# Projections of the second (HGRN2) layer: from float32 matmuls to three float32r products per weight tile

## The chip, the cores and the metric

One NeuronCore of a Trainium2 chip runs the whole program in one launch. The metric is the device time of one execution in microseconds. Five engines work in parallel, each on its own list of instructions, and meet at semaphores: PE (matrix multiply), DVE (VectorE), ACT (ScalarE), POOL (GpSimd) and SP, which here only issues transfers.

## The reference, cut to what matters

The reference chains four layers: an attention/convolution layer, an HGRN2 layer (below called layer 2), and a second block of two layers with feed-forward parts. The change touches the input projections of layer 2: 512 latent tokens and 256 context tokens of width 1024.

```python
def c_layer(x, xc, mod, mod_c, w_in, w_out, lb_f, lb_b, g_norm, ln_g, ln_b, ctx_out):
    widths = (C_F_WIDTH, C_F_WIDTH, C_F_WIDTH, C_I_WIDTH, C_I_WIDTH)      # five times 1024
    q, zf, zb, i, g = split_cols(modulate(x, shift, scale) @ w_in, widths)
    zfc, zbc, ic = split_cols(hc @ w_in[:, C_F_WIDTH:3 * C_F_WIDTH + C_I_WIDTH], ...)
    q = jax.nn.silu(to_heads(q, C_KEY_DIM)) * (C_KEY_DIM ** -0.5)
    o_f, oc_f = hgrn2_direction(q, i, zf, lb_f, qc, ic, zfc, ctx_out, reverse=False)
    o_b, oc_b = hgrn2_direction(q, i, zb, lb_b, qc, ic, zbc, ctx_out, reverse=True)
    y = hgrn2_readout(o_f + o_b, g, g_norm, w_out)
    x_new = layer_norm(DEEPNORM_ALPHA * x + gate * y, ln_g, ln_b)
```

`hgrn2_direction` takes log f = log sigmoid(z), its running sums along the tokens, and from their exponentials the keys, decays and scores of a linear recurrence, for 8 heads in both directions.

## The kernel before, in words

Tokens lie in tiles of 128; `HT` ("acts" in the profile) holds the modulated input transposed, 8 slices of 128 features by 768 tokens, and `X` ("resid") the residual rows. Weights come in chunks of 1024 x 256 float32 (1 MB) into `WR` ("weights_raw"), a ring of three slots; SP fills a slot when the chunk three places earlier is released.

Where this kernel already splits a product (the first layer, the second block), ACT or DVE rounds a chunk to float32r ("weights_hi"), POOL subtracts it from the raw chunk in place ("weights_lo"), and PE sums three products: hi by hi, hi by lo, lo by hi. The projections of layer 2 are not split before the change: one float32 matmul for each slice of 128 features. The trace records such a matmul as two.

Layer 2 has one step for each of the 8 heads (`STEPS`; two heads share a chunk of q or i). The projections are cut in units: `z` of a head has three (forward gate, backward gate, both for the context tokens), `q` two, `i` three, `g` two. In step `st` PE computes the three `z` units of the next head and two or three units of q, i or g, laid by halves between the recurrence's own work by `c_slots`: `between(0)` to `between(7)`. That work on PE is, in this order: transposes of the keys (L1084, "kt"), level 0 (L1013), `between(0)`, the outputs of the head before (L1020, L1033), states (L1099), the diagonal (L1107), level 1, `between(1)`, level 2, `between(2)`, then levels 3 to 6 with `between(3)` to `between(6)` behind them.

A level is a chain over four engines: POOL makes its arguments (`level_args`, three instructions, L2998 to L3000), ACT their exponential (L1673), DVE multiplies by keys and queries (L2304, L2305), PE multiplies (L1013) and DVE merges the result under a mask. The arguments have two buffers, so `level_args` of a level waits until PE has read the level two before.

The next head's gates form a second chain through the same engines, which starts when the last `z` unit is complete: ACT copies it out of PSUM (L1624) and takes a sigmoid (`keys`), DVE takes |z| (L2260), ACT an exponential and a logarithm (L1641, L1647), DVE forms log f (L2267) and four running sums (scans, L2273 to L2276) and signals `hg_sums` (L2280), ACT takes exponentials of them (`state_factors`, L1660 to L1669), DVE multiplies them by the keys (L2286, "h_z") and signals `hg_ks`, on which PE's kt of the next step waits. Every engine runs its list in the written order.

Of the kernel before, what the change touches and what calls it, by code (L numbers as in the profile page):

```python
# [48 lines left out]
def table_layout():  # L49

    sizes = [("ident", P), ("ones", P), ("pick", 2), ("win_lo", P), ("win_hi", P), ("dil", 1280),
             ("lv", P * len(LEVELS)), ("rot_ax", P), ("rot_pt", P),
             ("cos_ax", L), ("sin_ax", L), ("chunk", L), ("cols", 6)]
    at, out = 0, {}
    for name, n in sizes:
        out[name] = (at, at + n)
        at += n
    return out, at


def make_tables():
# [9 lines left out]
    put("pick", i[:, None] % 32 == np.arange(2)[None, :])  # L71
# [53 lines left out]
def program(nc, a, out, stop=99):  # L125
    lay, tw = table_layout()
    ctx = ExitStack()
    with ctx:
# [55 lines left out]
        chunks = []  # L184
# [18 lines left out]
        TAB_FIRST = lay["pick"][1]  # L203
# [5 lines left out]
        PICK = tab("pick")  # L209
# [14 lines left out]
        HKS = view(w + 19456, L, name="h_keys")  # L224
# [3 lines left out]
        HO = view(hi_at, TL, D, name="h_out")  # L228
# [9 lines left out]
        def c_slots(st):  # L238
# [8 lines left out]
            if st == LAST:  # L247
                share = (2, 2, 2, 2, 2, 0, 0, 0)
            else:
                share = (2, 2, 2, 1, 0, 2, 1, 0) if len(units) == 5 else (2, 2, 2, 1, 1, 2, 2, 0)  # L250
# [61 lines left out]
        Y_HI, Y_LO = parts("ab_out_hi", ht_at, KD, LT), parts("ab_out_lo", w + 4608, KD, LT)  # L312
        C_HI = parts("c_out_hi", w + 4096, KD, L)
# [224 lines left out]
        def _(pe):  # L538
# [10 lines left out]

            def chunk(pieces, kt=KD):  # L550

                n = len(chunks)
                s = n % WSLOTS
                chunks.append((pieces, kt))
                wcount[s] += 16 * len(pieces)
                pe.wait_ge(wload[s], wcount[s])
                return WR[:, s]
# [31 lines left out]
            def split_chunk(name, pieces, kt=KD, by="a"):  # L589
# [5 lines left out]
                w_hi, w_lo = OWN_HI[name] if name in OWN_HI else W_HI[:, len(splits) % 2], W_LO[n % WSLOTS]  # L595
# [4 lines left out]
                splits.append((n % WSLOTS, kt, w_hi, wload[n % WSLOTS], wcount[n % WSLOTS], by, hi_done, len(hi_list)))  # L600
# [365 lines left out]
            c_weights, c_release = {}, {}  # L966
# [6 lines left out]
            def product_half(unit, half):  # L973

                kind, key, part = unit
                if half == 0:
                    if part == 0:
                        c_weights[kind, key] = chunk(c_pieces(kind, key))
                        c_release[kind, key] = len(released)
                        released.append((None, 0))  # L980
# [4 lines left out]
                wv = c_weights[kind, key]  # L985
                ps = obank[n % 2]
                if kind in "zq" and part < 2:
# [3 lines left out]
                elif kind == "z":  # L991
                    for k in range(KD):
                        last = pe.matmul(ps[:, half * LC:(half + 1) * LC], wv[:, k, half * P:(half + 1) * P], HT[:, k, L:LT],
                                         start=k == 0, stop=k == KD - 1)
                else:
                    t = 2 * part + half
                    for k in range(KD):
                        last = pe.matmul(ps[:, half * WC:(half + 1) * WC], HT[:, k, t * P:(t + 1) * P], wv[:, k, :],  # L998
# [4 lines left out]
                if part == C_PARTS[kind] - 1:  # L1003
                    released[c_release[kind, key]] = (sem("products_filled"), n + 1)

# [37 lines left out]
            def turn_heads(hb, ps):  # L1043

                pe.wait_ge(sem("c_y"), hb + 1)
                for j in range(HH):
                    for t in range(TL):
                        h = HH * hb + j
                        last = pe.transpose(ps[:, j * L + t * P:j * L + (t + 1) * P], HO[:, t, h * P:(h + 1) * P], IDENT)
# [7 lines left out]
            product(("q", 0, 0))  # L1057
            pe.wait_ge(*read_of("h1.4"))
# [3 lines left out]
            mod_next(14)  # L1062
            product(("i", 0, 0))
            mod_next(15)
            product(("i", 0, 1))
            product(("i", 0, 2))
            mod_turn(1, 11)
            for st, (hb, hj) in enumerate(STEPS):
# [23 lines left out]
                pe.wait_ge(*product_emptied(("i", hb, 2)))  # L1092
# [292 lines left out]
        def _(sp):  # L1385
# [6 lines left out]
            for n, (pieces, kt) in enumerate(chunks):  # L1392
                if n == 10:
                    sp.dma_start(TAB[:, TAB_FIRST:tw], a["tables"][:, TAB_FIRST:tw]).then_inc(sem("tables_in"), 16)
                if n >= WSLOTS:
# [1765 lines left out]
```

## Time and profile before

| | us |
|---|---|
| median of 3 runs (2344.57 to 2349.4) | 2348.21 |
| the profiled execution, its own time | 2346.51 |
| its span in the trace | 2344.5 |
| PE busy in the span | 2151.1 (92%) |
| DVE, POOL, ACT busy | 1063.8, 810.5, 668.5 |
| mean granted TensorE clock | 0.97 |

Layer 2 begins with the product at 505.6 us of the span, its first step at 567.1, and its output product at 1055.2. A row of the timeline has the start and the duration of one instruction or of a run of like ones, the engine, the line of the program, what it writes and reads, and in brackets how long the engine stood idle before it and whom it waited for. Ends of matmuls are modelled and overlap the next start, so the pace of a run of matmuls is read from starts.

### The profile page before, as it was taken

To read this page: it belongs to the slowest core of one execution; us is meant where nothing else is said; L and a number is where in the kernel's file an instruction comes from. 1 tells how busy PE (TensorE), PEld (TensorE's weight loads), DVE (VectorE), ACT (ScalarE), POOL (GpSimd) and SP (SyncE) were. 2 spreads that over 40 slices of the span, in tenths; PEclk is the share of its full clock that TensorE was granted. 3 is DMA by queue.
4 is the path that set the end of the run, shared out by engine and by line. 5 is a ranking of instruction groups with operands and counts; after the bars stand their busy time and mean duration, and the time that the engine had idled before them with its cause. 6 is when DMAs were issued, how large, how long until landed. Compare 5 with 4: busy or idle time off the path is not lost. (4 is left out here: it accounts for less than half of the span.)

```text
span 2344.5 us, 27285 instructions
## 1 busy us (share of the span) xinstructions
PE 2151.1 (92%) x11287; PEld 1717.0 (73%) x11287; DVE 1063.8 (45%) x1685; ACT 668.5 (29%) x1043; POOL 810.5 (35%) x429
## 2 busy tenths in 40 slices
PE   4999888989898989987898899999998999999998
PEld 3887777866575757776855678888887688888886
DVE  2113664663555555557995543111126684111114
ACT  3223223334545454642112432100113353000111
POOL 1421113311333333325500015553544234554453
PEclk7999999999999999999899999999999999999999
DMA  9242113433111111113111112322322222232332
GB/s 300 72 116 74 55 55 91 126 109 90 36 36 36 36 36 37 36 55 99 41 36 54 55 54 72 105 93 91 107 90 90 83 97 72 90 108 90 93 96 81
DMA packets 183114, 187.41 MB, mean 80 GB/s; under 512 B 25728, under 2 KB 162256, under 8 KB 182864
## 3 DMA queue, kind: packets, MB, share of 16 engines
q1 hardware_dynamic: 173040, 175.42, 24.4%
q10 hardware_dynamic: 9376, 8.16, 1.3%
q8 instruction: 90, 1.47, 0.3%
q0 software_dynamic: 576, 2.10, 0.2%
q14 instruction: 32, 0.26, 0.0%
HBM read 183.56 MB, written 2.10 MB: 79 GB/s over the span
## 5 line engine op out<-in xcount | busy, mean ns | idle before, releaser
L3011 POOL TENSOR_TENSOR weights_lo<-weights_raw,weights_hi 128x2048 fp32r<-128x2048 f32 (+1 forms) x101 | 457.6, 4531 | 865.5 <-ACT weights_hi L1429 669.4
L698 PE MATMUL ring<-input_hi,weights_hi 128*128 128x512 f32 x784 | 305.4, 390 | 4.1 <-POOL weights_lo L3011 4.1
L700 PE MATMUL ring<-input_hi,weights_lo 128*128 128x512 f32 x784 | 305.0, 389 | 0.0
L699 PE MATMUL ring<-input_lo,weights_hi 128*128 128x512 f32 x784 | 305.0, 389 | 0.0
L2837 DVE CAST weights_hi<-weights_raw 128x2048 fp32r<-128x2048 f32 (+1 forms) x72 | 87.7, 1218 | 366.2 <-PE ring L700 173.9
L2998 POOL TENSOR_TENSOR h_w<-h_p 128x512 f32<-128x512 f32 x56 | 73.6, 1314 | 381.9 <-PE ring L1013 265.1
L989 PE MATMUL obank<-acts,weights_raw 128*128 128x512 f32 x384 | 179.6, 622 | 0.0
L698 PEld LDWEIGHTS ring<-input_hi,weights_hi 128*128 128x128 f32 x784 | 147.2, 188 | 36.4 <-issue 5.9
L700 PEld LDWEIGHTS ring<-input_hi,weights_lo 128*128 128x128 f32 x784 | 147.2, 188 | 30.5
L699 PEld LDWEIGHTS ring<-input_lo,weights_hi 128*128 128x128 f32 x784 | 147.2, 188 | 30.4
L998 PE MATMUL obank<-weights_raw,acts 128*128 128x256 f32 x640 | 142.7, 380 | 0.0
L989 PEld LDWEIGHTS obank<-acts,weights_raw 128*128 128x128 f32 x384 | 75.6, 203 | 87.2 <-issue 87.1
L1346 PE MATMUL ring<-weights_hi,hidden_hi 128*128 128x512 f32 x352 | 136.9, 389 | 0.0
L1347 PE MATMUL ring<-weights_lo,hidden_hi 128*128 128x512 f32 x352 | 136.9, 389 | 0.0
L1348 PE MATMUL ring<-weights_hi,hidden_lo 128*128 128x512 f32 x352 | 136.9, 389 | 0.0
L998 PEld LDWEIGHTS obank<-weights_raw,acts 128*128 128x128 f32 x640 | 120.3, 191 | 16.3 <-issue 0.8
L2858 DVE TENSOR_TENSOR f_gate<-f_gate,ring 128x1024 f32<-128x1024 f32 x22 | 26.9, 1221 | 212.4 <-PE ring L700 212.4
L3114 POOL TENSOR_TENSOR hidden_lo<-f_gate,hidden_hi 128x1024 fp32r<-128x1024 f32 x22 | 52.6, 2391 | 162.3 <-ACT hidden_hi L1925 162.3
L1013 PE MATMUL ring<-h_w 128*128 128x128 f32 x448 | 65.9, 293 | 46.0 <-DVE h_w L2305 25.0
L1013 PEld LDWEIGHTS ring<-h_w 128*128 128x128 f32 x448 | 59.2, 201 | 60.8 <-DVE h_w L2305 34.0
L1673 ACT ACTIVATE h_w<-h_w 128x1024 f32<-128x1024 f32 x56 | 58.5, 1053 | 131.2 <-POOL h_w L3000 131.0
L1925 ACT ACTIVATE hidden_hi<-f_gate 128x1024 fp32r<-128x1024 f32 x22 | 23.4, 1063 | 246.8 <-DVE f_gate L2858 246.8
(465 smaller groups left out, 4429.2 us busy)
## 6 DMA issues: line engine op xcount, KB each, us to landing
weights_raw<-in_w_ada SPq DMA_DIRECT2D x24, 1024.0 KB, 5.4
weights_raw<-in_ffn_w_gate SPq DMA_DIRECT2D x22, 1024.0 KB, 5.4
weights_raw<-in_ffn_w_up SPq DMA_DIRECT2D x22, 1024.0 KB, 5.4
weights_raw<-in_ffn_w_down SPq DMA_DIRECT2D x16, 1024.0 KB, 5.0
weights_raw<-in_w_in_c SPq DMA_DIRECT2D x12, 1024.0 KB, 5.2
weights_raw<-in_w_in_ab SPq DMA_DIRECT2D x9, 1024.0 KB, 7.2
weights_raw<-in_w_in_c SPq DMA_DIRECT2D x16, 512.0 KB, 5.3
weights_raw<-in_ev_w_in SPq DMA_DIRECT2D x8, 1024.0 KB, 5.5
```

Source lines behind the costliest of these rows:

```text
L698: pe.matmul(o, hi[:, k, ms], xh[:, k, t0:t0 + n], start=k == 0, stop=False)
L699: pe.matmul(o, hi[:, k, ms], xl[:, k, t0:t0 + n], start=False, stop=False)
L700: last = pe.matmul(o, lo[:, k, ms], xh[:, k, t0:t0 + n], start=False, stop=k == KD - 1)
L989: last = pe.matmul(ps[:, 0:L], wv[:, k, part * P:(part + 1) * P], HT[:, k, 0:L], start=k == 0, stop=k == KD - 1)
L998: last = pe.matmul(ps[:, half * WC:(half + 1) * WC], HT[:, k, t * P:(t + 1) * P], wv[:, k, :], start=k == 0, stop=k == KD - 1)
L1013: last = pe.matmul(ps[:, cs], W[:, 0, cs], W[:, 1, cs], start=True, stop=True)
L1346: pe.matmul(o, F_HI[f // 2][:, f % 2, ts], hi[:, k, :], start=f == 0, stop=False, skip_group_check=True)
L1347: pe.matmul(o, F_HI[f // 2][:, f % 2, ts], lo[:, k, :], start=False, stop=False, skip_group_check=True)
L1348: last = pe.matmul(o, F_LO[f // 2][:, f % 2, ts], hi[:, k, :], start=False, stop=end, skip_group_check=True)
L2837: dve.tensor_copy(w_hi[:, 0:kt, :], WR[:, slot, 0:kt, :]).then_inc(done, 1)
L2998: pool.tensor_tensor(w4[:, :, :, 0, :], refs.to_broadcast([P, 2, n, h2]), p4[:, :, :, 0, :], ALU.subtract)
L3011: pool.tensor_tensor(W_LO[slot][:, 0:kt, :], WR[:, slot, 0:kt, :], w_hi[:, 0:kt, :], ALU.subtract).then_inc(sem("w_lo"), 1)
```

## The change

The projections of layer 2 become sums of three float32r products, except those of `z` of head 0 and of `q` of heads 0 and 1.

- Weights: 18 chunks (`C_SPLIT`). `c_weights_hi(i)` on ACT rounds chunk i. Chunks of even number (i, q, g) are always loaded into the slot of the first of them, those of odd number (z, later g) into a second slot; the third slot holds the high parts of the odd ones. The high parts of the even ones lie in the part of the output `HO` that is not yet filled, and from number 12 on in two other places. `c_weights_lo(i)` on POOL subtracts in place. `chunk` is cut into `reserve` and the wait, and each chunk records its slot, its arrival count and who held the slot.
- Inputs: DVE casts the six tiles of `HT` to float32r (`C_XH` over the latent rows of `X`, `C_XH2` over tables); low parts go into `HT` itself, tiles 0 and 1 by DVE, tiles 2, 3 and the context by POOL, once the unsplit products have read it.
- `X` is therefore written to DRAM (`x_kept`, POOL's queue, 2 MB) and read back (SP's queue) behind the second chunk of the output weights.
- The mask table of a later attention ("dil") is loaded in the second block, not at the start.
- The first three units of i change order (the context's first), and in the last step the units of g are spread as 1, 1, 2, 2, 2, 2 halves over `between(0)` to `between(5)`, before as 2, 2, 2, 2, 2.

```diff
+            def c_weights_hi(i):
+                n = c_chunk[C_SPLIT[i]]
+                for before in (c_before[:2], c_before[2:])[i] if i < 2 else (c_chunk[C_SPLIT[i - 2]],):
+                    act.wait_ge(*released[before])
+                act.wait_ge(wload[slot_of[n]], arrival[n])
+                for k0, k1, home in c_hi_homes(i):
+                    act.activation(home[:, :, :], WR[:, slot_of[n], k0:k1, :], ACT.Copy).then_inc(sem("c_w_hi"), 1)
...
+            def c_weights_lo(i):
+                s = slot_of[c_chunk[C_SPLIT[i]]]
+                pool.wait_ge(sem("c_w_hi"), c_parts_made(i))
+                for k0, k1, home in c_hi_homes(i):
+                    pool.tensor_tensor(W_LO[s][:, k0:k1, :], WR[:, s, k0:k1, :], home[:, :, :], ALU.subtract).then_inc(sem("c_w_lo"), 1)
...
                 for st in range(len(STEPS)):
                     more = st + 1 < len(STEPS)
                     for i in range(2, 7):
                         level_args(7 * st + i)
+                        if i == (3 if more else 2):
+                            c_weights_lo(2 * st + 2)
+                        if i == (6 if more else 5):
+                            c_weights_lo(2 * st + 3)
...
+            def split_half(unit, half, ps):
...
+                if kind in "zq" and part < 2:
+                    for k in range(KD // 2 * half, KD // 2 * (half + 1)):
+                        ms = slice(part * P, (part + 1) * P)
+                        pe.matmul(ps[:, 0:L], c_hi(i, k)[:, ms], C_XH[:, :, k, :], start=k == 0, stop=False)
+                        pe.matmul(ps[:, 0:L], c_hi(i, k)[:, ms], C_XL[:, k, 0:L], start=False, stop=False)
+                        last = pe.matmul(ps[:, 0:L], lo[:, k, ms], C_XH[:, :, k, :], start=False, stop=k == KD - 1)
...
             product(("z", 0, 2))
             product(("q", 0, 1))
             mod_next(14)
+            pe.wait_ge(sem("c_in_lo"), 1)
+            product(("i", 0, 2))
+            mod_next(15)
+            pe.wait_ge(sem("c_in_lo_v"), 2)
             product(("i", 0, 0))
-            mod_next(15)
+            pe.wait_ge(sem("c_in_lo"), 3)
             product(("i", 0, 1))
-            product(("i", 0, 2))
...
+                if n == x_back_after[0]:
+                    for t in range(TL):
+                        sp.wait_ge(sem(f"x_kept{t}"), 16)
+                        sp.dma_start(X[:, t, :], X_KEPT[t]).then_inc(sem(f"x_back{t}"), 16)
```

POOL's list at the end of a step (h_p holds the running sums, h_w the levels' arguments; the last three h_w rows are level 6, the ones behind them level 0 of the next head). Before:

```order
L2998 TENSOR_TENSOR h_w33_81<-h_p31_79 128x512 [waits psum_filled]
L2999 TENSOR_TENSOR h_w33_81<-h_p31_79 128x256
L3000 TENSOR_TENSOR h_w33_81<-h_p31_79 128x256
L2998 TENSOR_TENSOR h_w32_80<-h_p30_78 128x8x64 [waits psum_filled,hg_sums]
L2999 TENSOR_TENSOR h_w32_80<-h_p30_78 128x4x64
```

After:

```order
L3136 TENSOR_TENSOR h_w33_81<-h_p31_79 128x512 [waits psum_filled]
L3137 TENSOR_TENSOR h_w33_81<-h_p31_79 128x256
L3138 TENSOR_TENSOR h_w33_81<-h_p31_79 128x256
L3172 TENSOR_TENSOR weights_lo1_145<-weights_raw9_57,c_w_hi2_156 128x2048 [waits c_w_hi]
L3136 TENSOR_TENSOR h_w32_80<-h_p30_78 128x8x64 [waits psum_filled,hg_sums]
L3137 TENSOR_TENSOR h_w32_80<-h_p30_78 128x4x64
```

One subtraction of 128 x 2048 stands between level 6 and the next head's level 0.

ACT's list over the same stretch, from the exponential of |z| to the exponentials of the sums. Before:

```order
L1641 ACTIVATE h_t26_74<-h_t26_74 128x1536 [waits hg_abs]
L1673 ACTIVATE h_w32_80<-h_w32_80 128x1024 [waits hg_warg]
L1647 ACT_TABLE_LOAD
L1647 ACTIVATE h_t26_74<-h_t26_74,tables1_49 128x1536 [waits hg_small]
L1673 ACT_TABLE_LOAD
L1673 ACTIVATE h_w33_81<-h_w33_81 128x1024 [waits hg_warg]
L1628 ACTIVATE h_i37_85<-obank0 128x512 [waits products_filled]
```

After:

```order
L1751 ACTIVATE h_t26_74<-h_t26_74 128x1536 [waits hg_abs]
L1783 ACTIVATE h_w32_80<-h_w32_80 128x1024 [waits hg_warg]
L1757 ACT_TABLE_LOAD
L1757 ACTIVATE h_t26_74<-h_t26_74,tables1_49 128x1536 [waits hg_small]
L1783 ACT_TABLE_LOAD
L1783 ACTIVATE h_w33_81<-h_w33_81 128x1024 [waits hg_warg]
L1745 ACTIVATE c_w_hi2_156<-weights_raw9_57 128x2048 [waits weights1,products_filled]
L1729 ACTIVATE h_i37_85<-obank0 128x512 [waits products_filled]
```

The rounding of the odd chunk stands behind level 6's exponential.

DVE's list ahead of the first step, behind the first head's logarithm. Before:

```order
L2276 SCALAR_TENSOR_TENSOR h_p30_78<-h_t26_74,tables1_49 128x255
L2278 COPY small4_52<-h_p30_78 128x6 [waits dve_chain]
L2279 TENSOR_TENSOR small4_52<-h_p30_78,h_t26_74 128x6
L2280 COPY small4_52<-small4_52 128x12 [waits dve_chain]
L2286 TENSOR_TENSOR h_z24_72<-h_z24_72,h_k28_76 128x1536 [waits hg_exps,hg_k]
```

After:

```order
L2409 SCALAR_TENSOR_TENSOR h_p30_78<-h_t26_74,tables1_49 128x255
L2411 COPY small4_52<-h_p30_78 128x6 [waits dve_chain]
L2412 TENSOR_TENSOR small4_52<-h_p30_78,h_t26_74 128x6
L2413 COPY small4_52<-small4_52 128x12 [waits dve_chain]
L2385 TENSOR_TENSOR c_in_lo_153<-acts8_56,c_in_hi_151 128x8x128 [waits products_filled] x2
L2419 TENSOR_TENSOR h_z24_72<-h_z24_72,h_k28_76 128x1536 [waits hg_exps,hg_k]
```

The two input subtractions, for which PE's product of i (tiles 0 and 1) waits, stand behind the scans.

## Rows read from the trace of the kernel before

**Rows 1.** Windows: window, its us, each engine's busy us; steps 4 and 5

```profile
807.34:865.79 58.45, 51.65 (x215) 33.18 (x214) 31.32 (x42) 25.90 (x34) 20.85 (x21) 0.94 0.12 36
865.79:927.53 61.74, 55.68 (x279) 43.36 (x278) 37.95 (x52) 30.55 (x40) 22.68 (x22) 1.00 0.12 35
```

**Rows 2.** Waits of PE, 480 to 1060 us: total, times, longest

```profile
PE ring L1013 <- DVE h_w L2305: 25.0, 18, 3.3
PE ring L1013 <- DVE h_states L2342: 20.9, 8, 3.0
```

**Rows 3.** Timeline of PE: one float32 unit each, 512 and 256 columns

```profile
809.32 7.03 PE L989 MATMUL obank<-acts,weights_raw 128*128 128x512 f32 x16
835.35 7.07 PE L993 MATMUL obank<-acts,weights_raw 128*128 128x256 f32 x32
```

**Rows 4.** Timeline of PE: float32r matmuls elsewhere, 512 columns, then 256

```profile
1399.67 0.40 PE L638 MATMUL ring<-weights_hi,e_out_hi 128*128 128x512 f32 x1
...
1402.87 0.39 PE L640 MATMUL ring<-weights_hi,e_out_lo 128*128 128x512 f32 x1
...
419.95 0.28 PE L884 MATMUL ring<-weights_hi,ab_out_hi 128*128 128x256 f32 x1
...
422.35 0.28 PE L886 MATMUL ring<-weights_hi,ab_out_lo 128*128 128x256 f32 x1
```

**Rows 5.** Timeline of ACT in step 4

```profile
838.03 1.06 ACT L1673 ACTIVATE h_w<-h_w 128x1024 f32<-128x1024 f32 x1 [2.78 <-POOL h_w L3000]
842.45 0.60 ACT L1624 ACTIVATE h_z<-obank 128x512 f32<-128x512 f32 x1 [3.37 <-PE obank L993]
850.96 1.57 ACT L1647 ACTIVATE h_t<-h_t,tables 128x1536 f32<-128x1536 f32 x1
853.85 1.06 ACT L1673 ACTIVATE h_w<-h_w 128x1024 f32<-128x1024 f32 x1
858.38 0.21 ACT L1660 ACTIVATE small<-small 128x12 f32<-128x12 f32 x1 [3.48 <-DVE small L2280]
```

**Rows 6.** Timeline of DVE in step 4

```profile
852.57 1.76 DVE L2267 SCALAR_TENSOR_TENSOR h_t<-h_z,h_t 128x1536 f32<-128x1536 f32 x1 [0.71 <-ACT h_t L1647]
856.08 1.20 DVE L2275 TENSOR_TENSOR_SCAN h_p<-h_t,tables 128x511 f32<-128x511 f32 x1
857.20 0.66 DVE L2276 TENSOR_TENSOR_SCAN h_p<-h_t,tables 128x255 f32<-128x255 f32 x1
859.94 1.10 DVE L2305 TENSOR_TENSOR h_w<-h_w,h_q 128x512 f32<-128x512 f32 x1
862.90 2.38 DVE L2286 TENSOR_TENSOR h_z<-h_z,h_k 128x1536 f32<-128x1536 f32 x1 [1.21 <-ACT h_t L1669]
```

**Rows 7.** Timeline of PE in steps 4 and 5: levels 1 and 6, kt, level 4

```profile
824.95 1.69 PE L1013 MATMUL ring<-h_w 128*128 128x128 f32 x8 [2.79 <-DVE h_states L2342]
861.47 1.05 PE L1013 MATMUL ring<-h_w 128*128 128x128 f32 x8
865.79 1.26 PE L1084 MATMUL ring<-tables,h_z 128*128 128x128 f32 x10
...
905.97 1.16 PE L1013 MATMUL ring<-h_w 128*128 128x128 f32 x8 [0.68 <-DVE h_w L2305]
```

**Rows 8.** Groups by form: total us, mean ns of one, idle before

```profile
L3011 POOL TENSOR_TENSOR weights_lo<-weights_raw,c_weights_hi 128x2048 fp32r<-128x2048 f32 x4 | 18.3, 4577 | 36.5 <-ACT c_weights_hi L1429 36.5
L1429 ACT ACTIVATE c_weights_hi<-weights_raw 128x2048 fp32r<-128x2048 f32 x4 | 7.6, 1902 | 0.0
```

**Rows 9.** Timeline of the second block: a subtraction on POOL, then a scan on DVE

```profile
1890.06 4.96 POOL L3011 TENSOR_TENSOR weights_lo<-weights_raw,weights_hi 128x2048 fp32r<-128x2048 f32 x1 [19.48 <-ACT weights_hi L1429]
1890.60 5.51 DVE L2960 TENSOR_TENSOR_SCAN r_xc<-r_a,r_gi 128x512 f32<-128x512 f32 x1
```

**Rows 10.** Timeline of PE and DVE ahead of step 0 and behind step 7

```profile
536.92 1.76 DVE L2260 SCALAR_TENSOR_TENSOR h_t<-h_z 128x1536 f32<-128x1536 f32 x1 [12.63 <-ACT h_z L1624]
...
567.12 1.29 PE L1084 MATMUL ring<-tables,h_z 128*128 128x128 f32 x10
```

More of the change, by code:

```diff
@@ L976, in product_half @@
                 if half == 0:
[L977 to L980, printed above, removed]
+                    if (kind, key) not in c_raw:
+                        c_ready(kind, key)
                     n = products[unit] = len(products)
@@ L984, in product_half @@
                 n = products[unit]
-                wv = c_weights[kind, key]
+                wv = c_raw[kind, key]
                 ps = obank[n % 2]
-                if kind in "zq" and part < 2:
+                if wv is None:
+                    last = split_half(unit, half, ps)
+                elif part < 2:
                     for k in range(KD // 2 * half, KD // 2 * (half + 1)):
@@ L990, in product_half @@
                                          start=k == 0, stop=k == KD - 1)
-                elif kind == "z":
+                else:
                     for k in range(KD):
                         last = pe.matmul(ps[:, half * LC:(half + 1) * LC], wv[:, k, half * P:(half + 1) * P], HT[:, k, L:LT],
[L994 to L998, printed above, removed]
                                          start=k == 0, stop=k == KD - 1)
@@ L1002, in product_half @@
                 last.then_inc(sem("products_filled"), 1)
[L1003 removed]
+                c_left[kind, key] -= 1
+                if c_left[kind, key] == 0:
                     released[c_release[kind, key]] = (sem("products_filled"), n + 1)
+            def split_half(unit, half, ps):
+                kind, key, part = unit
+                i = C_SPLIT.index((kind, key))
+                lo = W_LO[slot_of[c_chunk[kind, key]]]
+                if kind in "zq" and part < 2:
[4 more added lines that the diff above has]
+                        last = pe.matmul(ps[:, 0:L], lo[:, k, ms], C_XH[:, :, k, :], start=False, stop=k == KD - 1)
+                elif kind == "z":
+                    o, ms = ps[:, half * LC:(half + 1) * LC], slice(half * P, (half + 1) * P)
+                    for k in range(KD):
+                        pe.matmul(o, c_hi(i, k)[:, ms], C_XH2[:, :, k, :], start=k == 0, stop=False)
+                        pe.matmul(o, c_hi(i, k)[:, ms], C_XL[:, k, L:LT], start=False, stop=False)
+                        last = pe.matmul(o, lo[:, k, ms], C_XH2[:, :, k, :], start=False, stop=k == KD - 1)
+                else:
+                    t = 2 * part + half
+                    o = ps[:, half * WC:(half + 1) * WC]
+                    for k in range(KD):
+                        pe.matmul(o, c_x_hi(t, k), c_hi(i, k), start=k == 0, stop=False)
+                        pe.matmul(o, c_x_hi(t, k), lo[:, k, :], start=False, stop=False)
+                        last = pe.matmul(o, C_XL[:, k, t * P:(t + 1) * P], c_hi(i, k), start=False, stop=k == KD - 1)
+                return last
             def levels(st, i):
@@ L1732, in _ @@
                 level_exp(7 * st + 2)
+                if not more:
+                    c_weights_hi(2 * st + 2)
                 between(0)
@@ L1736, in _ @@
                 level_exp(7 * st + 3)
+                if more:
+                    c_weights_hi(2 * st + 2)
                 between(1)
```

154 lines of the change are left out of this document (123 added, 31 removed).

## The prediction, made before the changed kernel was run

> **What bounds the kernel now.** I read the windows by step first: a step of layer 2 takes 58.5 us where it has q units and 61.7 where it has i units, with PE busy 52 and 56 [rows 1]. So PE sets most of it, but not all. The waits of PE in the layer come to 25 us on the levels' operands and 21 us on the states [rows 2]. The timelines of ACT, DVE and PE in step 4 show why [rows 5 to 7]: the gate chain of the next head starts when ACT copies the last z unit (842.45), runs through |z|, exp and log (ends 852.5), log f and scans (852.57 to 857.9), `hg_sums` (858.3), six exponentials and h_z (862.90 to 865.3); kt begins at 865.79. Measured from the copy, S: `hg_sums` S+15.9, level 6 on PE S+19.0, kt S+23.3. PE's own work behind the last z unit of a q step (four levels at 0.9, four halves at 3.4) is 17 us. The end of a q step is therefore set by this chain and not by products. Step 5, with i units, has its kt at 927.5. Its copy lies 5 us ahead of level 4 at 905.97 [rows 7], at 901.1, so kt is at S+26.4: 3 us of slack over the chain.
>
> **The change, part by part.** All of it is summed against the profiled execution's own 2346.5 us (span 2344.5), 1.7 under the median 2348.2, which moves nothing below.
>
> *Products.* A float32 unit of 8 matmuls, 512 columns wide, takes 6.9 us by the pace of its starts; one of 16, 256 wide, 6.9 [rows 3]. Float32r matmuls start every 3.20/14 = 0.229 us at 512 columns and 2.40/20 = 0.120 at 256 [rows 4]. Three for one gives 24 x 0.229 = 5.5 and 48 x 0.120 = 5.8: 1.4 and 1.2 saved. Converted are 20 wide units (14 of z, 6 of q) and 27 narrow ones (7 z, 12 i, 8 g): 28 + 31 = 59 us, the whole gain if PE were the only bound.
>
> The Trainium skill would make this larger: "TensorE: Matmul & The Clock Gate", section "Back-to-back issue gap", has 131 ns for each matmul of 512 columns in a stream with weight loads. By it a wide unit would take 3.1 us and the first term would be 20 x 3.8 = 75 us in place of 28. The row says 0.229, and the row decides.
>
> *The copies.* Each step gets on ACT two roundings (1.9 us each) and on POOL two subtractions (4.6 each) [rows 8]. POOL has 38 us idle in a step, so by busy time they are free. But by the row of the second block a subtraction is not free for DVE: issued at 1890.06 and ended at 1895.0, it turned a scan issued at 1890.60 into 5.51 us, elsewhere 1.2 [rows 9]. The scan did nothing until POOL was done, although DVE was working when POOL asked: POOL gets in between two DVE instructions that follow each other directly.
>
> This is the rule that speaks against the change. The Trainium skill, "SBUF — State Buffer", section "SBUF: two separate sides", calls it an exclusive lock between GpSimd and a DVE instruction with two SBUF inputs, held for the whole instruction. The trace agrees with 5.51 against 1.2 us. If the two shared bandwidth instead, the term of 4.6 below would be near 2.3.
>
> *The even subtraction* (the q or i chunk, behind level 3's arguments) meets no two-input DVE work. It delays level 4's arguments, whose exponential stands on ACT ahead of the z copy. From level 1's start: its matmuls 1.7, arguments 2.9, exp 1.1, rounding 1.9, subtraction 4.6, arguments 2.5, exp 1.1: S is 15.8 behind level 1. Before it is 842.45 - 824.95 = 17.5 [rows 5, 7], and by products alone it could be 14.8 or less. So S is 1.7 earlier in a q step. In an i step, where the interval is about 15.9 and level 1 takes 1.1, it is 0.4 earlier.
>
> *The odd subtraction* (next z) needs the rounding behind level 6's exponential, which ends at 854.9. Its chunk is issued after the last z unit and lands 5.3 us later, in time. The rounding ends at S+14.4, or 856.8 in step 4. That is inside the third scan (856.08 to 857.28) and ahead of the fourth (857.20) [rows 6]. POOL takes the port at 857.3 and holds it to 861.9; the fourth scan waits. `hg_sums` moves by 4.6 us to S+20.5, and with it the exponentials, h_z and kt (S+27.9), level 6's operand (S+23.3; before, 861.04 is S+18.6), and level 0 behind.
>
> *A step.* The unit in `between(0)` lies on the path between level 0 and level 1: 1.4 saved. A q step: -1.4 - 1.7 + 4.6 = +1.5. An i step, and step 6 with its six units: level 6 at S+23.3, its matmuls 0.9 and a unit of 5.8 end at S+30.0 against S+26.4. That is +3.6. PE then comes from an idle of some 7 us. In step 4 a unit behind 3.3 us of idle took 1.5 us longer, at a mean granted clock of 0.94 against 1.00 in step 5 [rows 1]. I add 0.8, less than that one case: +3.6 + 0.8 - 0.4 - 1.4 = +2.6. Steps 0, 2, 4: +4.5. Steps 1, 3, 5, 6: +10.4.
>
> *Ahead of step 0.* POOL's context subtraction (128 x 2048, 4.6 us) starts as z's last unit ends, and |z| (536.92 [rows 10]) waits for it. POOL's two tile subtractions then hold up log f and a scan. Together `hg_sums` is 2.4 us later, DVE's two input subtractions (1.3 each, in turns with POOL) end near 558, and PE, through with `mod_next(15)` at 552, waits 6 us. Two units of i follow: kt at 571 against 567.1, +4. Bounds: +8 if the low parts come in later turns, -3 if nothing waits.
>
> *The last step.* The halves move behind later levels, and the even subtraction holds up DVE's h_sq, which eats the 4 us saved in `between(0)`. The g3 chunk can only be loaded once g1 is read, and its subtraction ends some 4 us after PE wants it. The output weights, before fetched early, now wait for g3's end: load 5.3, rounding 1.9, subtraction 4.6, about 12 us behind it. Before, the output product begins 11.9 us behind level 6. I take +1.3, between -5 (products alone) and +8 (each wait counted in full).
>
> *The rest.* 2 MB written to DRAM lie beside PE's transposes, and DVE needs them only at 524. Reading them back (7 us after the output weights) is due at 1083. The smaller table takes 0.65 MB from a start in which the DMA engines are full: -0.5. The two-slot ring costs nothing beyond what stands above, since each chunk has a third of a step to land.
>
> Sum: 4.5 + 10.4 + 4 + 1.3 - 0.5 = **+20 us**, 2366.
>
> **The rivals.**
> A. *PE is the bound throughout and the copies find gaps.* The 92% busy and the 0.9 of PE in most slices speak for it, the chain of 23 us in step 4 against it. 2346.5 - 59 = 2287.
> B. *The chain stands, but the subtractions cost DVE nothing*, because the rounding slips past the scans or POOL waits its turn. Then each step gains its three z units (4.0), an i step also its slack of 3: 7 x 4.0 + 4 x 3.0 = 40, with 6 of the last step and the first stretch: 2300. For it: POOL has the idle time. Against it: rows 9.
> C. *Half a collision.* The subtraction begins so that it overlaps the gaps of DVE at S+13 to S+16 or only a single short wait: 2.3 us and not 4.6. A q step is then -0.8, an i step +0.3, and with +4 and +1.3 the whole is within 4 us of before: 2350.
> B and A end on the other side. The mechanism that decides is one: who holds the port during the last scans. Below a delay of about 1.7 us of `hg_sums` per step the change gains.
>
> That the change does not do what it says would show as products still at 6.9 us; a float32r operand read in four blocks of 128 could be slower than 0.229, which would only add to the time (20 units x 1.4 = 28 us at most, were they as slow as before, of which a third is on the path).
>
> **How the numbers follow.** The forecast has 0.60, C 0.14, B 0.16, A 0.06, and 0.04 for something worse than 2385 (the products slow, or the weights late in the last step). Around the forecast I allow 12 us either way: the clock term, the first stretch and the last step. The range 2330 to 2382 leaves out A, B and the worse case and a little of the edges, and takes in C. A difference under 0.2% (4.7 us) can't be told from none. Slower by more: 0.60 + 0.04 less 0.02, and 0.03 of C: 0.65. Faster: A, B and 0.02 of C, 0.24. Within: 0.11.
>
> **What would show it.** Right: `weights_lo` beside the scans, with one scan of about 5 us in each step; `hg_sums` 20 us behind the z copy; PE idle 6 to 8 us ahead of level 6; units at 5.5 and 5.8 us; kt to kt near 60 and 64. Wrong: scans at their 0.7 and 1.2 us, kt to kt under 57, or PE without waits. The forecast is wrong if POOL is let in only when DVE's queue is empty.

## The result, and the profile after

| | before | after |
|---|---|---|
| median, us | 2346.39 (4 runs, 2344.3 to 2349.4) | 2374.14 (4 runs, 2371.59 to 2377.98) |
| profiled execution, us | 2346.51 | 2374.34 |
| its span, us; mean granted clock | 2344.5; 0.97 | 2372.5; 0.952 |

The changed kernel is slower: ratio 1.0119, 95% interval 1.0099 to 1.0138, or +23 to +32 us. The forecast was +20 and slower. Cut at the starts of kt and of the first and last product, the 28.0 us between the spans of the two profiled executions are:

| stretch | before | after | moved | forecast |
|---|---|---|---|---|
| start to the first product of layer 2 | 505.6 | 499.0 | -6.7 | -0.5 |
| first product to kt of step 0 | 61.5 | 66.5 | +5.0 | +4 |
| steps 0, 2, 4 | 56.5, 59.2, 58.5 | 60.6, 59.9, 61.1 | +7.6 | +4.5 |
| steps 1, 3, 5, 6 | 63.5, 61.1, 61.7, 61.6 | 64.2, 64.1, 64.4, 64.3 | +9.0 | +10.4 |
| step 7, to the output product | 66.1 | 77.1 | +10.9 | +1.3 |
| behind that | 1289.3 | 1291.4 | +2.1 | 0 |

The windows of steps 4 and 5 answer to [rows 1]: window, its us, then busy us of PE, weight loads, DVE, ACT and POOL, granted clock, share of the DMA engines, GB/s.

```profile
814.30:875.38 61.08, 48.26 (x265) 42.25 (x264) 34.91 (x45) 30.91 (x38) 30.08 (x23) 0.86 0.12 35
875.38:939.73 64.35, 52.10 (x360) 49.00 (x358) 39.41 (x51) 32.65 (x41) 31.52 (x24) 0.89 0.11 34
```

PE has 3.4 and 3.6 us less to do in a step, and the steps are 2.6 us longer. The clock fell from 0.94 and 1.00 to 0.86 and 0.89. PE's waits from 480 to 1090 us, which answer to [rows 2], say for what it stood:

```profile
PE ring L1103 <- DVE h_w L2438: 67.8, 21, 7.0
PE ring L1103 <- DVE h_states L2475: 23.5, 8, 5.7
PE ring L1139 <- DVE h_out L2525: 11.5, 1, 11.5
PE obank L1091 <- DVE c_in_lo L2385: 5.2, 1, 5.2
```

The waits for the levels' operands went from 25.0 to 67.8 us. The third row is the last step, the fourth the stretch ahead of step 0.

The gate chain of step 4, which answers to [rows 5, 6, 7]; ACT, POOL, DVE and PE in this order:

```profile
846.20 0.58 ACT L1725 ACTIVATE h_z<-obank 128x512 f32<-128x512 f32 x1
...
858.55 1.89 ACT L1745 ACTIVATE c_w_hi<-weights_raw 128x2048 fp32r<-128x2048 f32 x1
...
860.52 4.88 POOL L3172 TENSOR_TENSOR weights_lo<-weights_raw,c_w_hi 128x2048 fp32r<-128x2048 f32 x1 [5.79 <-ACT c_w_hi L1745]
...
859.82 1.19 DVE L2408 TENSOR_TENSOR_SCAN h_p<-h_t,tables 128x511 f32<-128x511 f32 x1
860.93 5.01 DVE L2409 TENSOR_TENSOR_SCAN h_p<-h_t,tables 128x255 f32<-128x255 f32 x1
...
870.98 1.76 DVE L2419 TENSOR_TENSOR h_z<-h_z,h_k 128x1536 f32<-128x1536 f32 x1 [1.21 <-ACT h_t L1779]
...
869.18 2.08 PE L1103 MATMUL ring<-h_w 128*128 128x128 f32 x8 [4.65 <-DVE h_w L2438]
...
875.38 1.25 PE L1181 MATMUL ring<-tables,h_z 128*128 128x128 f32 x10
```

POOL's subtraction is issued at 860.52, during the third scan. The fourth is issued at 860.93 and takes 5.01 us for 0.66: the subtraction ends at 865.40, the scan 0.54 us behind it. It is the same in each of the steps 0 to 6 (4.95 to 5.01). From the z copy (S) `hg_sums` comes at S+20.1 (866.26 in DVE's timeline), level 6 at S+23.0 and kt at S+29.2. Level 6 itself takes 2.08 us for 1.05: it runs at half clock behind its wait. The clock over this stretch, in windows of 4 us (window, us, PE busy, clock, DMA share, GB/s):

```profile
850.30:854.30 4.00, 1.16 (x8) 0.96 0.00 0
854.30:858.30 4.00, 2.97 (x11) 0.50 0.00 0
858.30:862.30 4.00, 4.00 (x13) 0.69 0.01 2
862.30:866.30 4.00, 2.22 (x10) 1.00 0.00 0
866.30:870.30 4.00, 1.12 (x5) 0.66 0.00 0
870.30:874.30 4.00, 4.00 (x13) 0.50 0.00 0
```

Behind the wait of 3.31 us ahead of level 5 (855.3) and that of 4.65 ahead of level 6 PE is granted 0.50, its level of 1.2 GHz, for a window or more, and works at half pace.

The products answer to [rows 3, 4]; two matmuls of a wide unit, three places apart in PE's timeline:

```profile
820.86 0.39 PE L1080 MATMUL obank<-c_in_hi,weights_lo 128*128 128x512 f32 x1
...
821.54 0.39 PE L1080 MATMUL obank<-c_in_hi,weights_lo 128*128 128x512 f32 x1
```

That is 0.227 us each, 5.4 us for the 24 of a unit.

DVE ahead of step 0, which answers to [rows 10] (|z|, then the two input subtractions), and the end of the last step:

```profile
530.82 5.63 DVE L2393 SCALAR_TENSOR_TENSOR h_t<-h_z 128x1536 f32<-128x1536 f32 x1 [9.03 <-ACT h_z L1725]
...
547.52 3.20 DVE L2385 TENSOR_TENSOR c_in_lo<-acts,c_in_hi 128x1024 fp32r<-128x1024 f32 x2
```

```profile
1047.19 0.55 PE L1091 MATMUL obank<-c_w_hi,c_in_hi 128*128 128x256 f32 x1 [4.78 <-issue]
...
1041.86 5.23 POOL L3172 TENSOR_TENSOR weights_lo<-weights_raw,c_w_hi 128x2048 fp32r<-128x2048 f32 x1 [2.97 <-ACT c_w_hi L1745]
...
1067.75 1.91 ACT L1530 ACTIVATE c_weights_hi<-weights_raw 128x2048 fp32r<-128x2048 f32 x1 [5.21 <-DMA weights_raw<-in_w_out_c]
1069.57 2.10 ACT L1803 ACTIVATE c_out_hi<-ring,small 128x1024 fp32r<-128x1024 f32 x2
...
1069.74 4.51 POOL L3149 TENSOR_TENSOR weights_lo<-weights_raw,c_weights_hi 128x2048 fp32r<-128x2048 f32 x1 [20.36 <-ACT c_weights_hi L1530]
1070.80 1.28 DVE L2532 SCALAR_TENSOR_TENSOR c_out_lo<-ring,small,c_out_hi 128x1024 fp32r<-128x1024 f32 x1 [8.02 <-ACT c_out_hi L1803]
...
1076.38 1.94 PE L1139 MATMUL ring<-tables,h_out 128*128 128x128 f32 x8 [11.47 <-DVE h_out L2525]
...
1081.11 0.47 PE L680 MATMUL ring<-c_weights_hi,c_out_hi 128*128 128x512 f32 x1 [1.40 <-DVE c_out_lo L2532]
```

The first row is PE's wait for the parts of g3 (the last chunk of g): the profile names nobody for it, but POOL's subtraction of that chunk ends at 1047.09, and PE goes on at 1047.19.

In the last step ACT stands at the rounding of the first output weights until they have landed. Behind it in ACT's list are the copies of the heads (L1803), whose banks are full by then. DVE waits 8.0 us for them, PE's next turn of heads 11.5, and the output product begins at 1081.1, 18.2 us behind level 6. Before it was 11.9:

```profile
1043.35 1.06 PE L1013 MATMUL ring<-h_w 128*128 128x128 f32 x8
...
1055.24 0.47 PE L638 MATMUL ring<-c_weights_hi,c_out_hi 128*128 128x512 f32 x1 [1.08 <-DVE c_out_lo L2399]
```

### The profile page after: what moved, and what is told of

Its sections match the earlier page's. It is cut to its first block and busy times, and to the rows that moved or that the text cites. A ratio compares the mean times of both kernels' runs of the same rounds, so it can differ in the third digit from the quotient of the medians.

```text
span 2372.5 us, 28558 instructions
## 1 busy us (share of the span) xinstructions
PE 2117.6 (89%) x11879; PEld 1766.7 (74%) x11879; DVE 1102.5 (46%) x1693; ACT 698.4 (29%) x1062; POOL 912.5 (38%) x457
## 5 line engine op out<-in xcount | busy, mean ns | idle before, releaser
L1103 PE MATMUL ring<-h_w 128*128 128x128 f32 x448 | 77.2, 326 | 91.3 <-DVE h_w L2438 67.8
L1103 PEld LDWEIGHTS ring<-h_w 128*128 128x128 f32 x448 | 68.0, 230 | 99.3 <-DVE h_w L2438 73.9
L1530 ACT ACTIVATE weights_hi<-weights_raw 128x2048 fp32r<-128x2048 f32 x32 | 61.2, 1912 | 91.0 <-DMA weights_raw<-in_w_in_ab 51.4
L740 PE MATMUL ring<-ab_in_hi,weights_hi 128*128 128x512 f32 (+1 forms) x224 | 78.1, 349 | 9.3 <-POOL ab_in_lo L3155 9.3
L1092 PE MATMUL obank<-weights_lo,c_in_hi 128*128 128x256 f32 x256 | 77.0, 301 | 0.0
L2043 ACT ACTIVATE f_gate<-ring 128x1024 f32<-128x1024 f32 x22 | 22.7, 1031 | 183.8 <-PE ring L742 173.8
```

What stands on the lines that cost most here:

```text
L740: pe.matmul(o, hi[:, k, ms], xh[:, k, t0:t0 + n], start=k == 0, stop=False)
L1092: pe.matmul(o, c_x_hi(t, k), lo[:, k, :], start=False, stop=False)
L1103: last = pe.matmul(ps[:, cs], W[:, 0, cs], W[:, 1, cs], start=True, stop=True)
L1530: act.activation(w_hi[:, 0:kt, :], WR[:, slot, 0:kt, :], ACT.Copy).then_inc(done, 1)
```

## The experiments

All are edits of the changed kernel unless said. "Step sum" is the time from kt of step 0 to kt of step 7: 422.0 us before, 438.6 after. Ratios are against the kernel before as measured beside the experiment: 2345.77 (1 to 4), 2344.28 (5 to 8), 2346.55 (9 to 11) and 2343.51 (12). So differences of 2 or 3 us across these groups mean little.

**1. The odd subtraction left out** in steps 0 to 5. Its place is kept with 8 columns, and the products read the high part twice.

```diff
+                m = 8 if i % 2 and 3 <= i < 15 else WC
...
-                    pool.tensor_tensor(W_LO[s][:, k0:k1, :], WR[:, s, k0:k1, :], home[:, :, :], ALU.subtract).then_inc(sem("c_w_lo"), 1)
+                    pool.tensor_tensor(W_LO[s][:, k0:k1, 0:m], WR[:, s, k0:k1, 0:m], home[:, :, 0:m], ALU.subtract).then_inc(sem("c_w_lo"), 1)
```

> Changed kernel, but in steps 0 to 5 the odd subtraction on POOL (the next z chunk's low part) is cut to 8 columns per row block, and the products read the high part in the low part's place: PE, ACT and DMAs have the same work. Theory (the subtraction holds DVE's port through the last scan, in the gate chain): the scan at 0.7 us in place of 5.0, hg_sums 16 us behind the z copy, and six steps shorter by 3.5 to 4.6 us each, so 21 to 28 us off 2374: 2346 to 2353. Rival (the lengthening is PE's granted clock and the ACT rounding; the scan's delay is covered by PE's products): under 5 us off. Step 6, where the subtraction stays, keeps its length in both.

Measured: 2345.19 (11 runs), 0.9991 of before (0.9982 to 1.0001), 29 us under the changed kernel. The fourth scan in step 4:

```profile
842.44 0.74 DVE L2410 TENSOR_TENSOR_SCAN h_p<-h_t,tables 128x255 f32<-128x255 f32 x1
```

Steps 0 to 5 are 54.1, 59.6, 54.3, 61.1, 54.3, 61.3: 3.0 to 6.8 less each. Step 6 kept the subtraction and its 63.7. The theory holds and the rival falls: six subtractions of 4.6 us cost 29 us. The q steps gain 5.7 to 6.8 us, more than the subtraction lasts, because level 6 then also runs at full clock (1.16 us for 2.08). The i steps gain 3.0 to 4.6, because the next level 0 then waits for its operand (3.5 us behind kt for 1.1 to 2.2).

**2. The even subtraction left out** in steps 0 to 5, by the same edit with `i % 2 == 0 and 2 <= i < 14`.

> Changed kernel, but in steps 0 to 5 the even subtraction on POOL (the q or i chunk, behind level 3's arguments) is cut to 8 columns and the high part is read twice; nothing else differs. My theory has this subtraction in the chain ahead of the z copy in q steps: without it the copy comes when the unit z.2 is through on PE (845.0 in step 4 where the copy was at 846.2), so 1 to 1.5 us per q step and nothing in i steps: 3 to 5 us off 2374. Rival 1 (it delays level 4's arguments by a full 4.6 us which no other work covers): 10 us or more off. Rival 2 (hidden altogether): no difference.

Measured: 2365.65 (2363.28 to 2366.95), ratio 1.0087 (1.0073 to 1.0101), 8.5 us off. That is between the theory and rival 1. The step sum is 428.6. Four of the six steps are 2.1 to 2.8 us shorter, i steps too, where the expectation gave nothing; step 5 is 0.6 shorter and step 2 is 1.2 longer, where level 1 takes 2.05 us for 1.44 and the copy comes later than with the subtraction.

**3. The odd subtraction behind the next head's arguments.**

```diff
-                        if i == (6 if more else 5):
-                            c_weights_lo(2 * st + 3)
...
                         level_args(7 * st + 7)
                         level_args(7 * st + 8)
+                        c_weights_lo(2 * st + 3)
```

> Changed kernel; in steps 0 to 6 POOL makes the odd subtraction behind the arguments of the next head's levels 0 and 1, not ahead of its wait for hg_sums. All work is as in the changed kernel. Theory: the scans run free, hg_sums at S+16; the subtraction then lies at about S+20 to S+25, where DVE has h_z and the next head's first level operands: kt is at S+24 to S+27 and the first z unit of the next step may wait 1 to 2 us for it. 1.5 to 4 us off per step: 2350 to 2364. Rival (what the scans gain, h_z and the operands lose, since POOL takes the port for 4.6 us wherever it stands): within 5 us of 2374, with one operand of some 4 to 5 us in each step in the place of the scan.

Measured: 2377.9 (2375.62 to 2378.05), ratio 1.0138 (1.0124 to 1.0152). Nothing gained, as the rival said, and its mechanism is there at the start of step 3, on DVE and then PE:

```profile
747.41 3.90 DVE L2437 TENSOR_TENSOR h_w<-h_w,h_k 128x512 f32<-128x512 f32 x1 [1.53 <-ACT h_w L1783]
```

```profile
751.97 2.08 PE L1103 MATMUL ring<-h_w 128*128 128x128 f32 x8 [5.37 <-DVE h_w L2438]
```

The scans run in 0.66 us, but level 0's operand now waits for POOL (3.90 for 0.68), and in steps 1 to 6 level 1 comes 20.6 to 24.6 us behind kt where it came at 16.1 to 17.4. Steps 1 to 5 together are 1.5 us shorter. Step 0, whose subtraction now falls into step 1, is 6.6 shorter, and step 6, which needs g1's low part within itself, takes 72.2 us, 7.9 longer.

**4. Heads ahead of the late output weights** on ACT, in the last step.

```diff
-            hi_upto("y10.0")
             act.wait_ge(sem("gn_in"), 16)
             heads_hi(0)
             heads_hi(1)
+            hi_upto("y10.0")
             heads_hi(2)
```

> Changed kernel; on ACT the rounding of the output weights' first chunk (which waits for weights loaded only behind g3's products) stands behind the copies of heads 0 and 1 and ahead of the copies of the third pair, where it stood ahead of all three. Theory (ACT's program order keeps the heads' copies, and with them DVE's heads, PE's turn and the output product, waiting for the late weights): the output product begins some 7 us earlier (1074 for 1081), when the weights' subtraction ends; 5 to 8 us off 2374. Rival (the late weights themselves are the bound, and the heads come in their shadow): under 1.5 us off.

Measured: the output product 70.5 us behind the last kt for 77.1, so the 6.6 us are there. It now waits for the weights themselves:

```profile
1080.82 0.77 PE L680 MATMUL ring<-c_weights_hi,c_out_hi 128*128 128x512 f32 x1 [3.52 <-POOL weights_lo L3149]
```

The whole took 2371.32 (2369.65 to 2373.84), only 2.8 us under the changed kernel, with ranges that overlap: the gain is seen in the stretch and not in the whole. Its profiled execution had 6 us more ahead of the first product, in code that the edit does not touch.

**5. Both subtractions left out** in steps 0 to 6, by the same edit with `2 <= i < 16`.

> Changed kernel, but both subtractions on POOL in steps 0 to 6 are cut to 8 columns and the products read the high part twice; ACT's roundings, the DMAs and PE's work stay. This is what the float32r products alone are worth, with the copies' second half free. Theory (two separate places in the chain: even 8.5 us together, odd 29 us together, and 5 more from step 6, which kept both before): the savings add up, 2374 - 43 = 2331 (2326 to 2338). Rival (PE or the wait for the states takes over once one of the two is gone): 2338 to 2345. In both, far above the 2287 that 59 us of saved products would give.

Measured: 2335.02 (2331.51 to 2338.77), ratio 0.9955 (0.9942 to 0.9969). The savings add up to 39 us, 4 less than expected. The step sum is 403.9, so with subtractions that cost nothing the steps gain 18 us on the kernel before.

**6. The products alone undone.**

```diff
-                        pe.matmul(ps[:, 0:L], c_hi(i, k)[:, ms], C_XH[:, :, k, :], start=k == 0, stop=False)
-                        pe.matmul(ps[:, 0:L], c_hi(i, k)[:, ms], C_XL[:, k, 0:L], start=False, stop=False)
-                        last = pe.matmul(ps[:, 0:L], lo[:, k, ms], C_XH[:, :, k, :], start=False, stop=k == KD - 1)
+                        last = pe.matmul(ps[:, 0:L], f(lo[:, k, ms]), f(C_XL[:, k, 0:L]), start=k == 0, stop=k == KD - 1)
```

> Changed kernel with all roundings, subtractions and DMAs, but each unit of the split chunks is multiplied once in float32 (low part by low part, a product that means nothing) in place of three float32r matmuls, so PE's part of the change alone is undone. Theory (the units ahead of the z copy are on the path, those behind it stand in the shadow of the gate chain): the z copy some 3.2 us later (35 us behind kt in place of 32) and between levels 6 and kt a unit of 6.9 for 5.8 in i steps, so 3.2 to 4.5 us per step and 2 to 5 in the last and first stretches: 2374 + 27 to 38, 2400 to 2412. Rival (the chain covers the products everywhere): within 5 us of 2374.

One float32 product of the two low parts stands in the place of the three for each slice of features; the sum of three is left out, and all copies stay.

Measured: 2407.62 (2405.26 to 2411.52), ratio 1.027 (1.0256 to 1.0283). So the products take 33 us off, and all the rest of the change (roundings, subtractions, transfers, order) adds 61, both with what the clock does in them (0.962 in the mean here, 0.952 in the changed kernel). In the step sum they are +42.7 and -26.1.

**7. Both subtractions on DVE** in steps 0 to 6.

```diff
                 level_scores(st, 2)
+                if more:
+                    c_weights_lo_v(2 * st + 2)
...
                 level_operand(7 * st + 6)
+                if more:
+                    c_weights_lo_v(2 * st + 3)
                 level_scores(st, 5)
```

POOL's list loses these fourteen and keeps those of the first two and the last two chunks.

> Changed kernel; in steps 0 to 6 both subtractions are done by DVE: the even one behind level 2's scores, ahead of |z|, the odd one behind level 6's operand, ahead of level 5's scores. The last step and the first stretch stay. Theory (it was the port held through the last scan, and POOL's queue of arguments, that cost the time, and not the work): about 2.5 us each, both in DVE's idle time; scan at 0.7 us, level 6 some 19 us and kt 23 us behind the z copy; 2333 to 2343. Rival (DVE's own 2.5 us lands in the chain as POOL's 4.6 did, and holds POOL's next arguments too): half of the gain, 2350 to 2360.

Measured: 2337.2 (2329.37 to 2341.38), ratio 0.9963 (0.9949 to 0.9977): faster than before. The odd one in step 4, in DVE's pause ahead of h_z:

```profile
844.87 2.70 DVE L2545 TENSOR_TENSOR weights_lo<-weights_raw,c_w_hi 128x2048 fp32r<-128x2048 f32 x1
...
848.26 1.85 DVE L2419 TENSOR_TENSOR h_z<-h_z,h_k 128x1536 f32<-128x1536 f32 x1
```

The same subtraction is 2.7 us on DVE and 4.6 on POOL. It is somewhat longer than the pause: h_z starts 6.2 us behind `hg_sums`, 4.7 in experiment 5. The step sum is 405.6, against 403.9 with none at all in experiment 5.

**8. And the last step mended:** experiments 4 and 7, with the output weights loaded into the slot that g2 leaves.

```diff
+            next_slot[0] = slot_of[c_chunk["i", 0]]
             last_heads = take("cy3", "v")
```

> The kernel before this one in the list, and two changes in the last step: ACT copies heads 0 and 1 ahead of rounding the first output weights, and these weights are loaded into the slot that g2 leaves, not the one that g3 leaves. Theory: with the first alone the output product came 70.5 us behind the last kt in place of 77.1, held by the weights' subtraction; with the second it is held by the third pair of heads only and comes 65 to 68 us behind kt. 9 to 12 us below the kernel before this one: 2323 to 2334, faster than the kernel before the change. Rival (PE's g3 units and their copies bound it): 6.6 us only.

Measured: 2331.73 (2326.06 to 2335.47), ratio 0.994 (0.9927 to 0.9954). That is 5.5 us below experiment 7, where 9 to 12 were expected. The last step is 69.2 us for 76.7, between theory and rival.

**9. Input subtractions ahead of log f,** and the rounding of the output weights back ahead of the heads: an edit of the kernel of 8.

```diff
             abs_z(0)
-            log_f_and_sums(0)
+            dve.wait_ge(sem("c_in_hi"), 6)
             c_in_lo(0)
             c_in_lo(1)
+            log_f_and_sums(0)
...
+            hi_upto("y10.0")
             act.wait_ge(sem("gn_in"), 16)
             heads_hi(0)
             heads_hi(1)
-            hi_upto("y10.0")
```

> The kernel of the run before (subtractions of the steps on DVE, output weights in g2's slot), with two moves: DVE subtracts its two input tiles ahead of log f of head 0, in its idle time, and not behind the scans; and ACT rounds the first output weights ahead of all heads again, since they now come early. Theory: ahead of step 0 PE no longer waits 5.2 us for c_in_lo, and the first kt comes 61 to 63 us behind the first product in place of 66; in the last step POOL is through with the first output weights before the heads and the output product comes 66 to 68 us behind kt in place of 69.2. 2332 - 4 to 7: 2325 to 2328. Rival for the first (log f, the scans and with them level 0 come later by what DVE and POOL share): nothing gained. Rival for the second (the rounding holds the heads' copies up as before): 2 us lost.

Measured: 2329.96 (2327.42 to 2336.33), ratio 0.9933 (0.9918 to 0.9949); not to be told from the one above. Both rivals have a part. kt comes 58.5 us behind the first product, 7.5 sooner, but level 0 then waits and step 0 grows by 4.3. The last step is 72.1, 2.9 longer.

**10, 11. Filler matmuls** (whose results are overwritten) in PE's waits, to see what the half clock costs; on the kernel of 9, then on the changed kernel. `q` and `other` stand for the number of matmuls ahead of each level, in steps 0, 2, 4 and in the others.

```diff
-                pe.wait_ge(sem("hg_w"), 7 * st + i + 1)
                 ps = take(f"lv{st}.{i}", "v")
+                for _ in range((q if st in (0, 2, 4) else other).get(i, 0)):
+                    pe.matmul(ps[:, 0:L], C_XL[:, 0, 0:P], C_XL[:, 0, 0:L], start=True, stop=True)
+                pe.wait_ge(sem("hg_w"), 7 * st + i + 1)
```

> The kernel one above, and PE gets float32r matmuls of 512 columns (0.229 us each at full clock) that mean nothing, into the bank that the level's own overwrite: in each step 10 ahead of level 1, 4 ahead of level 4, 12 (q steps) or 1 (i steps) ahead of level 5, 3 or 8 ahead of level 6, each lot about as long as the wait for the operand there. Theory (a wait is followed by some 4 us of half clock, and ahead of the z copy these are on the path): level 1 at 1.1 us for 1.7, no stretch under 0.9 of clock in a step, z copy 1 to 2 us earlier: 1 to 3 us per step, 2308 to 2320. Rival (the clock falls elsewhere, or the filler ends behind the operand and takes what the clock gives): within 4 us of the kernel above, or slower.

> The changed kernel, everything in its place, with the same kind of filler matmuls: 10 ahead of level 1, 7 (q steps) or 6 (i steps) ahead of level 4, 12 ahead of level 5 in q steps, 16 or 18 ahead of level 6. Theory (my term of 0.8 us for an i step: PE comes from an idle of 5 to 7 us and does level 6 and the unit behind it at half clock): level 6 at 1.16 us for 2.08 and kt 2 to 4 us earlier in i steps and step 6, the z copy 1 to 1.6 earlier in every step, kt of q steps else unchanged since h_z sets it: 2354 to 2366. Rival (the gate chain alone sets the steps, the clock costs nothing): within 4 us of 2374.

Measured: 2339.61 (9 runs) and 2394.45 (4 runs), 10 and 20 us slower. Neither expectation held, in part because of how I placed them: the wait ahead of level 1 is for its PSUM bank, so the ten matmuls stood behind it, and on the changed kernel level 1 came 2.3 to 4.3 us later. The step sums grew by 3.3 and 13.5 us. On the changed kernel a wait of 2.8 to 2.9 us was left ahead of level 6 in i steps and step 6, and level 6 still took 2.08. The wholes tell nothing of what the clock costs. One row does, the ten matmuls behind the wait in step 4 on the changed kernel:

```profile
842.99 4.63 PE L1100 MATMUL ring<-c_in_lo 128*128 128x512 f32 x10 [2.69 <-DVE h_states L2477]
```

The granted clock from 843.0 to 847.4 was 0.50. At the 0.227 us of the products the ten would take 2.3.

**12. Filler ahead of level 6 alone,** 17 or 26 matmuls.

> The changed kernel with filler float32r matmuls (512 columns, the bank that level 6 overwrites) ahead of level 6 alone: 17 in steps 0, 2 and 4 (3.9 us at full clock, PE idle there 4.65 in step 4), 26 in the other steps (6.0 us, idle there 5.6 to 7.0). The lots at level 1, 4 and 5, of which that at level 1 stood behind the wait and not in it, are gone. Theory (the half clock behind the wait lengthens level 6 and the unit behind it, which is the path in i steps and step 6): level 6 at 1.2 us for 2.08, from level 6 to kt 7 us for 9.2 in those four steps, 1 to 2.5 us less each, so 4 to 10 us off: 2364 to 2370; steps 0, 2 and 4, where h_z sets kt, within 0.5 us. Rival (the clock costs nothing there, or the filler runs past the operand): 2372 to 2380.

Measured: 2368.07 (2365.39 to 2375.52), ratio 1.0107 (1.0061 to 1.0153). The whole tells little by that interval; the trace tells more. Level 6 of step 5 and the kt behind it:

```profile
929.41 1.16 PE L1105 MATMUL ring<-h_w 128*128 128x128 f32 x8
936.10 1.26 PE L1183 MATMUL ring<-tables,h_z 128*128 128x128 f32 x10
```

That is 6.7 us from level 6 to kt, in steps 1, 3, 5 and 6, for 8.4 to 9.5 in the changed kernel. In steps 0, 2 and 4 it is 4.0 for 5.2 to 6.3, where I expected no change. Part is given back: level 0 comes up to 3.6 us behind kt, for 1.1 to 2.2, since its operand is not ready. The step sum is 433.6, 5.0 less.

## Why the prediction was right, point by point

- **POOL's subtraction holds DVE's port through the fourth scan: right, and shown.** Forecast `hg_sums` at S+20.5 and level 6 at S+23.3; measured S+20.1 and S+23.0. Experiment 1 takes it away, and 29 us go. Rivals B and C fall with it. The Trainium skill, "SBUF — State Buffer", section "SBUF: two separate sides", has this as an exclusive lock, and the trace agrees: the scan is held to the subtraction's end (865.40) and then done within 0.54 us, not slowed throughout.
- **Products 5.5 and 5.8 us, 1.4 less a unit: right.** The z copy comes 31.9 us behind kt for 35.1, where I had 3.1 sooner. By experiment 6 the products give 33 of their 59 us, and rival A falls.
- **Even subtraction: its chain right, its price too small.** The copy was forecast 15.8 us behind level 1 in a q step and about 15.5 in an i step (by the prediction's own terms 15.2); it comes at 15.7 in step 4 and 15.9 in step 5. But by products alone I had 14.8, and without the subtraction it comes as early as 13.3 (steps 0, 1 and 3 of experiment 2), 14.7 and 14.9 in steps 4 and 5. It costs 8.5 us in six steps.
- **q steps +1.5: too small, by clock.** I let the clock lengthen only i steps (0.8 us). In q steps level 6 and the half unit behind it also run at half clock, and they, not h_z, set kt: h_z ends at 872.7, kt starts at 875.4. Experiment 12 gets 1.2 to 2.3 us of that back in a q step, and 1.7 to 2.8 in the others.
- **i steps and step 6, +2.6 each: near in sum, by two errors that offset.** They moved by +0.7, +3.0, +2.6 and +2.7. From the copy to kt it is 31.3 to 32.5 us for 26.55, so +4.7 to +5.9 where I had +4.4: the 0.8 for the clock was too small. Level 6 to kt takes 8.4 to 9.5 us, where I had 6.7 and that 0.8, and with PE kept busy ahead of it (experiment 12) it took just the 6.7. Against this the copy comes 1.7 to 4.9 us sooner behind kt, where I had 1.8. That the two nearly cancel is luck.
- **Ahead of step 0, +4: right** (+5.0), with PE's wait of 5.2 us for DVE's input subtractions as told.
- **The last step, +1.3: this is the term that failed;** it measured +10.9. Of that, 4.7 us are up to level 6, where PE waits 4.8 for g3's parts, which I had told but set against a saving; h_sq is held up as told (3.39 us for 0.69). The other 6.3 lie between level 6 and the output product. I counted load, rounding and subtraction behind g3's end, and that sum was right: the subtraction ends at 1074.25, 12 us behind g3. But I did not count that ACT's rounding of these weights stands ahead of the heads' copies in its list, so the output product begins only at 1081.1. Experiment 4 moves it and gets 6.6 us back.
- **The start, -0.5:** measured -6.7, most of which need not be the change's. In the profiled executions of the twelve experiments, whose code there is that of the changed kernel, the first product starts between 497.0 and 505.4, at the latest nearly where it did before. One place goes with it: from 325 to 350 us the granted clock was 0.80 before and 1.00 after. Among the thirteen with the change the start is 497.0 to 500.1 where it was 1.00 there, 500.7 and 501.4 where it was 0.93, and 501.1 to 505.4 where it was 0.80. What the change itself does to the start stays open, with one trace of the kernel before. The rows are window, us, busy us by engine, clock, DMA share and GB/s, before and then after:

```profile
325.00:350.00 25.00, 22.48 (x146) 17.83 (x147) 14.73 (x37) 6.46 (x16) 4.55 (x1) 0.80 0.27 84
```

```profile
325.00:350.00 25.00, 20.38 (x161) 16.42 (x160) 16.41 (x40) 6.98 (x16) 4.57 (x1) 1.00 0.27 85
```

So the forecast was right in sign and in its main mechanism, and its number came near in part by luck: in these two executions the shorter start hid two thirds of what I missed in the last step. Left open are the 2.1 us behind the output product (1.6 to 4.0 in all kernels with the change). That the products' gain in an i step is almost nothing even without subtractions (62.1 us in step 5 of experiment 5, 61.7 before) goes with half clock in part. Behind the same wait of 2.15 us level 0 took 1.16 us in step 1 of that run (granted clock 1.00 from 619 to 623), with level 1 15.2 us behind it, and 2.07 and 2.04 us in steps 3 and 5 (0.57 from 733 to 737 and from 849 to 853), with level 1 16.8 behind it. No run takes that wait away.

## What to carry to other kernels

Before work goes to an idle engine, look at which instruction of another engine it will block and whether that one is in the chain: here the 4.6 us of "free" POOL time for the odd subtraction cost as much as they lasted (29 us for six), and with both subtractions on DVE, largely in its pauses, the steps together were only 1.7 us longer than with none. An added wait on an engine is priced by all that stands behind it in that engine's list, the roundings of late weights too. And time taken from PE where a chain sets the step comes back as waits, behind which PE is slower.

## What the runs showed of the hardware

- POOL is let in between two DVE instructions that follow each other without a gap, and DVE's next one with two SBUF inputs then waits out the whole subtraction (0.66 us became 5.01). It goes the other way too: with the odd subtraction on DVE, a row of POOL's arguments took 2.25 us for 1.05 beside it (step 4 of experiment 7).
- PE's waits of 3.31 and 4.65 us in step 4 were followed by windows of 4 us at a granted clock of 0.50, and with the wait ahead of level 6 filled by matmuls, level 6 took 1.16 us for 2.08. Ten float32r matmuls set behind a wait of 2.69 us took 4.63 us at a granted clock of 0.50 (step 4 of experiment 11), where 0.227 us each would make 2.3.
